# A seven-product matmul kernel: one of the four weight-block sums of each unit made by an accumulating DMA on Pool's queue

## The chip, the cores and the metric

One core of a Trainium2 chip runs the whole program. The metric is the device time of one execution in microseconds. Before the change the median of three runs is 978.04 us (976.92 to 979.71).

## The reference

The reference is a two-layer model of 256 tokens with 1024 features, all in float32. Each layer is a token mixer, a layer norm, a mixture of 16 experts and a second layer norm. Only the input projection of the first mixer matters here:

```python
def _mixer_ab(x, pos, w_in, ...):
    proj = x @ w_in          # [256, 1024] @ [1024, 6152]
    rq, rk, rv, rg, mq, mk, mv, mo, mi, mf = _split(proj, RET_SPLITS + ML_SPLITS)
    ...                      # retention on rq..rg, mLSTM on mq..mf
    return y @ w_out
```

## The kernel before, in words

The 6144 wide columns of this projection are cut into twelve units of 512 columns, ab0 to ab11. A unit's weights are 2 MB. SyncE (SP) loads them in two halves of 1 MB (rows 0 to 511, then 512 to 1023, L577 and L578) into one of six slots of `ring`, with the semaphores `ring_full` and `ring_rest`. A slot is loaded again when the unit in it has been used up (`freed`). The MoE weights follow through the same ring later on.

ab0 and ab1 (queries and keys of the retention, which VectorE then rotates by position, `rotate`) are multiplied in the plain way. ab2 to ab11 are the *seven-product units*: tokens (two blocks of 128) by inner dimension (two halves of 512) and inner dimension by columns (two blocks of 256) form 2x2 blocks, and seven block products take the place of eight, after Strassen and Winograd. A block product is 4 matmul calls of 128x256, or 8 of 128x128 in the two units whose result is kept with features on the partitions; the trace shows two instructions for each call. The blocks of a unit's weights are W11 (rows 0 to 511, columns 0 to 255), W12 (the same rows, columns 256 to 511), W21 and W22 (the rows below).

For each unit VectorE makes four sums of weight blocks, each one TENSOR_TENSOR of 128x1024. Three are in `mix_weights`: sums[1] = W22 - W12 (L2072), W12 := W12 - W11 in the slot itself (L2073), sums[0] = W22 - (the new W12) (L2076). The fourth is `mix_last` (L2083): W21 := W21 - sums[0], after the product of the old W21. Four sums of token blocks (`mix_tokens`, L2059, 128x512 each) are made once for all units: numbers 0 and 2 after the rotation of ab0, numbers 1 and 3 after that of ab1. `mix_weights` of ab2 stands between the two halves of the rotation of ab1.

TensorE's order in a unit (L813 for most units, L816 for the two of the other layout): the first product, W11 with the first token block (`first_product`, which is issued inside the unit before); then in `other_products` W21 with the first token block; sums[0] with token_mix[1]; sums[1] with token_mix[2]; W12 with token_mix[0]; the next unit's first product (`gap`); W22 with token_mix[3]; the corrected W21 with the second token block. Between products ScalarE copies the running sums out of the bank (`first_copy`, `sum_copy`, L1622) and VectorE adds the bank of another product to a copy (`blend`, L2095), in three steps for each unit. Semaphores carry this: `weights_mixed` (four for each unit), `tokens_mixed`, `product_done`, `first_copied`, `copied`, `combined`.

Every engine works through its program in order, and the order is written out by hand. On VectorE it is: rotate ab0, mix_tokens(0, 2), first half of rotate ab1, mix_weights(ab2), second half of rotate ab1, mix_tokens(1, 3), the gates of the mLSTM (from L2130), then for each unit blend 0, mix_last, blend 1, mix_weights of the next unit, blend 2, with the attention work of the finished heads between them. For ab6 and ab7 mix_weights of the next unit stands ahead of blend 1. ScalarE takes the Exp and Ln of the gates ahead of the first `sum_copy` of ab2.

GpSimd (POOL) has only DMAs on its queue in this stretch: parameter rows at L699 and L702, issued by 17.4 us, and then, after `y_done` has reached 8, the loads of the layer norm's rows (L725, L726), which are issued at 199.4 us.

Of the kernel before, what the change touches and what calls it, by code (L numbers as in the profile page):

```python
# [9 lines left out]
ALU = mybir.AluOpType  # L10
# [3 lines left out]
P = 128  # L14
SEQ = 256
# [87 lines left out]
def build(nc, a, out):  # L103
    with ExitStack() as ctx:
# [3 lines left out]
        def sem(name):  # L108
            return ctx.enter_context(nc.semaphore(name))
# [176 lines left out]
        tokens_mixed = sem("tokens_mixed")  # L286
        weights_mixed = sem("weights_mixed")
        first_done = sem("first_done")
        product_done = sem("product_done")
# [263 lines left out]
        def wait_unit(eng, name, t=None):  # L553

            eng.wait_ge(combined, 3 * fast[name] + (1 if t == 0 else 3))
            if t != 1:
                eng.wait_ge(copied, 3 * fast[name] + 3)

        block = ctx.enter_context(nc.Block())

# [136 lines left out]
        def _(pool):  # L697
# [3 lines left out]
            for dst, src in par_list[2:PAR_FIRST]:  # L701
                pool.dma_start(dst, src).then_inc(rows_in, 16)  # L702
            lns = [("ln_mix_g", "ln_mix_b", 0), ("ln_ffn_g", "ln_ffn_b", 0),
                   ("ln_mix_g", "ln_mix_b", 1), ("ln_ffn_g", "ln_ffn_b", 1)]
# [31 lines left out]
        def _(pe):  # L736
# [101 lines left out]
            def other_products(name, n, fill=None, gap=None):  # L838
# [8 lines left out]
                if fill:  # L847
                    fill()
                pe.wait_ge(weights_mixed, 4 * unit + 3)
                pe.wait_ge(tokens_mixed, 3)  # L850
# [4 lines left out]
                if unit:  # L855
                    pe.wait_ge(combined, 3 * unit)
                product(name, 2, token_mix[2], sums[1], True)
                pe.wait_ge(copied, 3 * unit + 1)
                product(name, 0, token_mix[0], weight_block(n, 0, 1), False).then_inc(product_done, 1)
                if gap:  # L860
# [3 lines left out]
                product(name, 0, token_mix[3], weight_block(n, 1, 1), False).then_inc(product_done, 1)  # L864
                pe.wait_ge(weights_mixed, 4 * unit + 4)
                pe.wait_ge(combined, 3 * unit + 2)
# [743 lines left out]
        def _(act):  # L1610
# [10 lines left out]
            def fn(o, i, f, **kw):  # L1621
                return nc.scalar.activation(o, i, f, **kw)  # L1622
# [18 lines left out]
            def first_copy(name):  # L1641

                act.wait_ge(first_done, fast[name] + 1)
                if name == "ab8":
                    act.wait_ge(weights_mixed, 4 * fast["ab7"] + 4)
                fn(place(name, 0, 0), held_part(name, 0), ACT.Copy).then_inc(first_copied, 1)

            def sum_copy(name, *which):

                for i in which:  # L1650
                    act.wait_ge(product_done, 5 * fast[name] + (2, 3, 4)[i])
                    fn(place(name, *((1, 0), (1, 1), (0, 1))[i]), held_part(name, 0), ACT.Copy).then_inc(copied, 1)

# [338 lines left out]
        def _(dve):  # L1992
# [58 lines left out]
            def mix_tokens(*which):  # L2051

                half = lambda t, kh: hT[:, 4 * kh:4 * kh + 4, t * P:(t + 1) * P]
                terms = ((half(1, 0), half(1, 1), ALU.add, 0), (token_mix[0], half(0, 0), ALU.subtract, 1),
                         (half(0, 0), half(1, 0), ALU.subtract, 0), (half(0, 1), token_mix[1], ALU.subtract, 3))
                for i in which:
                    x, y, op, done = terms[i]
                    dve.wait_ge(tokens_mixed, done) if done else None
                    V.tensor_tensor(token_mix[i], x, y, op).then_inc(tokens_mixed, 1)  # L2059

            def unit_weights(name):
                return ring[:, unit_no(0, int(name[2:])) % RING, :].rearrange("p (k n) -> p k n", k=KC)

            def mix_weights(name):

                unit, w, sums = fast[name], unit_weights(name), mixes(name)
                n = unit_no(0, int(name[2:]))
                dve.wait_ge(ring_full[n % RING], landed(n))
                dve.wait_ge(ring_rest[n % RING], landed(n))
                if unit:  # L2070
                    dve.wait_ge(product_done, 5 * unit - 2)
                V.tensor_tensor(sums[1], w[:, 4:8, SEQ:], w[:, 0:4, SEQ:], ALU.subtract).then_inc(weights_mixed, 1)  # L2072
                V.tensor_tensor(w[:, 0:4, SEQ:], w[:, 0:4, SEQ:], w[:, 0:4, 0:SEQ], ALU.subtract) \  # L2073
                    .then_inc(weights_mixed, 1)
                dve.wait_ge(weights_mixed, 4 * unit + 2)
                V.tensor_tensor(sums[0], w[:, 4:8, SEQ:], w[:, 0:4, SEQ:], ALU.subtract).then_inc(weights_mixed, 1)  # L2076

            def mix_last(name):

                unit, w, sums = fast[name], unit_weights(name), mixes(name)  # L2080
                dve.wait_ge(product_done, 5 * unit + 1)
                dve.wait_ge(weights_mixed, 4 * unit + 3)
                V.tensor_tensor(w[:, 4:8, 0:SEQ], w[:, 4:8, 0:SEQ], sums[0], ALU.subtract).then_inc(weights_mixed, 1)  # L2083

            def blend(name, *which):

                unit = fast[name]
                for i in which:
# [5 lines left out]
                    o = place(name, *((0, 0), (1, 1), (1, 0))[i])  # L2094
                    V.tensor_tensor(o, o, held_part(name, 1 if i == 0 else 2), ALU.add).then_inc(combined, 1)  # L2095

# [770 lines left out]
```

## Time and profile before

| what | value |
|---|---|
| median of three runs | 978.04 us (976.92 to 979.71) |
| the profiled execution, its time | 975.02 us |
| its span, first to last instruction | 973.1 us |
| TensorE matmuls busy | 940.3 us, 97% of the span |
| weight loads of TensorE | 549.6 us, 56% |
| VectorE | 358.4 us, 37% |
| ScalarE | 233.2 us, 24% |
| GpSimd | 15.2 us, 2% |
| granted TensorE clock, mean | 0.998 of full speed |
| DMA in the queues of SP, of Pool | 271.60 MB, 6.53 MB |

The profile is of one execution, and its own time, not the median of the runs, is what its rows add up to. TensorE's matmuls are pipelined, so a busy TensorE row says little about gaps; the idle time ahead of the weight loads (PEld) says more. An instruction's idle time is listed with what ended it, its releaser. A DMA has an issue time on the queue that starts it, and a time from issue to landing.

### The profile page before, as it was taken

To read this page: it belongs to the slowest core of one execution; us is meant where nothing else is said; L and a number is where in the kernel's file an instruction comes from. 1 tells how busy PE (TensorE), PEld (TensorE's weight loads), DVE (VectorE), ACT (ScalarE), POOL (GpSimd) and SP (SyncE) were. 2 spreads that over 40 slices of the span, in tenths; PEclk is the share of its full clock that TensorE was granted. 3 is DMA by queue.
4 is the path that set the end of the run, shared out by engine and by line. 5 is a ranking of instruction groups with operands and counts; after the bars stand their busy time and mean duration, and the time that the engine had idled before them with its cause. 6 is when DMAs were issued, how large, how long until landed. Compare 5 with 4: busy or idle time off the path is not lost.

```text
span 973.1 us, 10781 instructions
## 1 busy us (share of the span) xinstructions
PE 940.3 (97%) x4272; PEld 549.6 (56%) x4272; DVE 358.4 (37%) x847; ACT 233.2 (24%) x497; POOL 15.2 (2%) x29
## 2 busy tenths in 40 slices
PE   9999999999999999999999999999999999999996
PEld 8888988744533453333585568887545333443322
DVE  4666686523422121120335344644225220131204
ACT  1123353310311120110303353433513111111101
POOL 2000000000000000000000000000000000000001
PEclk9999999999999999999999999999999999999999
DMA  8984433453799999999995233444546899999994
GB/s 276 338 295 140 171 124 137 184 205 140 298 395 423 421 422 421 402 419 416 391 327 192 87 131 129 173 140 191 189 172 260 351 418 421 420 422 419 419 419 168
DMA packets 65782, 278.87 MB, mean 287 GB/s; under 512 B 8852, under 2 KB 9216, under 8 KB 41920
## 3 DMA queue, kind: packets, MB, share of 16 engines
q1 hardware_dynamic: 63856, 271.60, 71.1%
q0 software_dynamic: 1872, 6.53, 1.9%
q8 instruction: 37, 0.61, 0.2%
q14 instruction: 17, 0.14, 0.0%
HBM read 277.04 MB, written 1.06 MB: 286 GB/s over the span
## 4 chain that ended last, share of the span: by engine, by line
PE 79%; DMA 15%; DVE 3%; issue 1%; ACT 1%; SPq 0%; DVEq 0%
PE bank L746 63%; DMA ring<-in_moe_w_up 12%; PE bank L813 10%; DMA ring<-in_moe_w_down 2%; PE bank L1192 2%; PE bank L816 2%; DMA ring<-in_w_in_ab 1%; PE bank L1554 1%; PE bank L1197 1%; PE bank L905 1%; DVE feat L2280 1%; PE bank L1099 0%; ACT feat L1622 0%; PE bank L1140 0%; DVE stat L2589 0%
## 5 line engine op out<-in xcount | busy, mean ns | idle before, releaser
L746 PE MATMUL bank<-ring,feat 128*64 128x512 f32 (+1 forms) x1152 | 228.6, 595 | 3.0 <-ACT feat L1622 2.7
L746 PE MATMUL bank<-ring,hT 128*64 128x512 f32 (+1 forms) x544 | 161.0, 596 | 8.9 <-DMA ring<-in_moe_w_up 5.5
L746 PEld LDWEIGHTS bank<-ring,feat 128*64 128x64 f32 (+1 forms) x1152 | 74.2, 131 | 142.6 <-issue 131.0
L1622 ACT ACTIVATE feat<-bank 32x512 f32<-32x512 f32 (+3 forms) x128 | 60.8, 494 | 385.4 <-PE bank L746 241.3
L746 PE MATMUL bank<-hT,ring 128*128 128x256 f32 x640 | 140.1, 379 | 0.2 <-DMA ring<-in_w_in_ab 0.2
L746 PEld LDWEIGHTS bank<-hT,ring 128*128 128x128 f32 x640 | 121.8, 191 | 16.4 <-DMA ring<-in_w_in_ab 0.6
L746 PE MATMUL bank<-ring,yT 128*128 128x512 f32 x256 | 112.8, 595 | 0.0
L746 PEld LDWEIGHTS bank<-ring,hT 128*64 128x64 f32 (+1 forms) x544 | 59.3, 149 | 93.9 <-issue 87.1
L2579 DVE COPY feat<-bank 32x512 f32<-32x512 f32 (+1 forms) x56 | 38.5, 687 | 145.9 <-PE bank L746 145.4
L746 PEld LDWEIGHTS bank<-ring,yT 128*128 128x128 f32 x256 | 47.9, 190 | 55.3 <-issue 55.1
L2569 DVE TENSOR_TENSOR feat<-feat,bank 128x512 f32<-128x512 f32 x16 | 11.0, 688 | 172.7 <-PE bank L746 172.7
L1622 ACT ACTIVATE tok<-bank 128x256 f32<-128x256 f32 (+1 forms) x52 | 22.3, 431 | 133.7 <-PE bank L813 71.2
L813 PE MATMUL bank<-ring,hT 128*128 128x256 f32 x192 | 44.6, 380 | 0.0
L813 PEld LDWEIGHTS bank<-ring,hT 128*128 128x128 f32 x192 | 36.2, 190 | 5.6 <-issue 0.8
L746 PEld LDWEIGHTS bank<-tok,h 128*128 128x128 f32 x128 | 32.5, 331 | 11.4 <-issue 11.1
L746 PE MATMUL bank<-tok,h 128*128 128x256 f32 x128 | 37.6, 429 | 0.9 <-DVE tok L2456 0.9
L1622 ACT ACT_TABLE_LOAD x25 | 32.1, 1283 | 2.2 <-PE bank L746 1.7
L2291 DVE SCALAR_TENSOR_TENSOR feat<-bank,cols_cd,feat 128x255 f32<-128x255 f32 (+2 forms) x48 | 23.1, 481 | 25.7 <-ACT feat L1622 24.6
L1192 PE MATMUL bank<-feat 128*128 128x512 f32 x64 | 30.9, 607 | 1.0 <-ACT feat L1622 1.0
L813 PE MATMUL bank<-ring,yT 128*128 128x256 f32 x128 | 30.2, 379 | 0.0
L813 PEld LDWEIGHTS bank<-ring,yT 128*128 128x128 f32 x128 | 24.1, 190 | 3.1
L2095 DVE TENSOR_TENSOR tok<-tok,bank 128x256 f32<-128x256 f32 x30 | 12.5, 418 | 27.6 <-ACT tok L1622 21.5
(276 smaller groups left out, 802.5 us busy)
## 6 DMA issues: line engine op xcount, KB each, us to landing
ring<-in_moe_w_up SPq DMA_DIRECT2D x60, 1024.0 KB, 16.8
ring<-in_moe_w_gate SPq DMA_DIRECT2D x56, 1024.0 KB, 13.3
ring<-in_moe_w_down SPq DMA_DIRECT2D x56, 1024.0 KB, 12.1
ring<-in_w_in_ab SPq DMA_DIRECT2D x24, 1024.0 KB, 9.0
ring<-in_w_in_cd SPq DMA_DIRECT2D x24, 1024.0 KB, 13.6
ring<-in_w_out_ab SPq DMA_DIRECT2D x8, 1024.0 KB, 6.1
ring<-in_moe_w_down SPq DMA_DIRECT2D x16, 512.0 KB, 17.5
ring<-in_w_out_cd SPq DMA_DIRECT2D x8, 1024.0 KB, 6.0
```

The lines of the kernel that those rows point to most:

```text
L746: return nc.tensor.matmul(o, l, r, start=start, stop=stop)
L813: last = nc.tensor.matmul(o, x[:, k, :], y[:, k, :], start=first and k == 0, stop=k == 3, skip_group_check=True)
L816: last = nc.tensor.matmul(o[:, cols], y[:, k, cols], x[:, k, :], start=first and m == 0 and k == 0, stop=k == 3, skip_group_check=True)
L905: last = nc.tensor.transpose(bank[b][:, k * SEQ + t * P:k * SEQ + (t + 1) * P], src[:, t, c * P:(c + 1) * P], ident)
L1192: return nc.tensor.matmul(bank[4 + 2 * t + q][:, :], selw_t[:, t, :], ye[:, t, q * 512:(q + 1) * 512], start=start, stop=False, skip_group ...
L1197: last = nc.tensor.transpose(bank[0][:, c * P:(c + 1) * P], hid[:, c:FF:FF // P], ident)
L1554: last = nc.tensor.matmul(bank[b][e * SSD_HD:(e + 1) * SSD_HD, c * SEQ + j * P:(c + 1) * SEQ], xdt[:, j, hd * SSD_HD:(hd + 1) * SSD_HD], p ...
L1622: return nc.scalar.activation(o, i, f, **kw)
L2095: V.tensor_tensor(o, o, held_part(name, 1 if i == 0 else 2), ALU.add).then_inc(combined, 1)
L2291: ins = V.scalar_tensor_tensor(out=o, in0=bank[b][:, (m % 2) * SEQ:(m % 2 + 1) * SEQ - back], scalar=cols[:, c:c + 1], in1=o, op0=ALU.mult ...
L2569: V.tensor_tensor(hid, sil, bank[3][:, :], ALU.mult) \
L2579: ins = V.tensor_copy(ye[r, t, 512:1024], bank[3][r, :])
```

## The change

Pool's queue gets ten accumulating DMAs, one for each of ab2 to ab11, behind its parameter rows. When both halves of a unit's weights have landed, the DMA reads the W11 block (512 rows, 256 columns, 512 KB) once more from the input in device memory and adds it to the W12 block in the slot. Two semaphores `added`, used in turn, tell of it; from the third addition on Pool also waits for the one two before. `mix_weights` waits for `added` instead of the two ring semaphores and has two sums: sums[0] = W22 + W12', sums[1] = sums[0] - W11, where W12' is the block with W11 added. `mix_last` adds instead of subtracting. So that the signs come out right, the token sums become SCALAR_TENSOR_TENSOR with a factor of -1 (L2059), two of the three `sum_copy` of a unit copy with a scale of -1, and one `blend` of the three subtracts. `weights_mixed` now counts three for each unit. TensorE waits for the first sum ahead of the product with sums[0], for the second ahead of the product with sums[1], and for `added` ahead of the product with W12'.

```diff
@@ -285,6 +285,7 @@
         fix_ready = sem("fix_ready")
         tokens_mixed = sem("tokens_mixed")
         weights_mixed = sem("weights_mixed")
+        added = [sem(f"added{i}") for i in range(2)]
         first_done = sem("first_done")
         product_done = sem("product_done")
         first_copied = sem("first_copied")
@@ -556,6 +557,12 @@
             if t != 1:
                 eng.wait_ge(copied, 3 * fast[name] + 3)
 
+        def unit_weights(name):
+            return ring[:, unit_no(0, int(name[2:])) % RING, :].rearrange("p (k n) -> p k n", k=KC)
+
+        def wait_added(eng, name):
+            eng.wait_ge(added[fast[name] % 2], 16 * (fast[name] // 2 + 1))
+
         block = ctx.enter_context(nc.Block())
 
 
@@ -700,6 +707,20 @@
             pool.wait_ge(ring_rest[0], 16)
             for dst, src in par_list[2:PAR_FIRST]:
                 pool.dma_start(dst, src).then_inc(rows_in, 16)
+            def add_blocks(name):
+
+                unit, n = fast[name], unit_no(0, int(name[2:]))
+                pool.wait_ge(ring_full[n % RING], landed(n))
+                pool.wait_ge(ring_rest[n % RING], landed(n))
+                if unit > 1:
+                    pool.wait_ge(added[unit % 2], 16 * (unit // 2))
+                source, c0 = AB_UNITS[int(name[2:])]
+                pool.dma_start(unit_weights(name)[:, 0:4, SEQ:],
+                               a[source][0, 0:D // 2, c0:c0 + SEQ].rearrange("(k p) n -> p k n", p=P),
+                               accum_op=ALU.add).then_inc(added[unit % 2], 16)
+
+            for n in range(2, 12):
+                add_blocks(f"ab{n}")
             lns = [("ln_mix_g", "ln_mix_b", 0), ("ln_ffn_g", "ln_ffn_b", 0),
                    ("ln_mix_g", "ln_mix_b", 1), ("ln_ffn_g", "ln_ffn_b", 1)]
             for n, (g, b, l) in enumerate(lns):
@@ -846,7 +867,7 @@
                 product(name, 1, token_block(0, 1), weight_block(n, 1, 0), True).then_inc(product_done, 1)
                 if fill:
                     fill()
-                pe.wait_ge(weights_mixed, 4 * unit + 3)
+                pe.wait_ge(weights_mixed, 3 * unit + 1)
                 pe.wait_ge(tokens_mixed, 3)
                 pe.wait_ge(first_copied, unit + 1)
                 product(name, 0, token_mix[1], sums[0], False).then_inc(product_done, 1)
@@ -854,15 +875,17 @@
                     pe.wait_ge(stored[2], plan[name][2])
                 if unit:
                     pe.wait_ge(combined, 3 * unit)
+                pe.wait_ge(weights_mixed, 3 * unit + 2)
                 product(name, 2, token_mix[2], sums[1], True)
                 pe.wait_ge(copied, 3 * unit + 1)
+                wait_added(pe, name)
                 product(name, 0, token_mix[0], weight_block(n, 0, 1), False).then_inc(product_done, 1)
                 if gap:
                     gap()
                 pe.wait_ge(copied, 3 * unit + 2)
                 pe.wait_ge(tokens_mixed, 4)
                 product(name, 0, token_mix[3], weight_block(n, 1, 1), False).then_inc(product_done, 1)
-                pe.wait_ge(weights_mixed, 4 * unit + 4)
+                pe.wait_ge(weights_mixed, 3 * unit + 3)
                 pe.wait_ge(combined, 3 * unit + 2)
                 product(name, 2, token_block(1, 1), weight_block(n, 1, 0), False).then_inc(product_done, 1)
 
@@ -1642,14 +1665,15 @@
 
                 act.wait_ge(first_done, fast[name] + 1)
                 if name == "ab8":
-                    act.wait_ge(weights_mixed, 4 * fast["ab7"] + 4)
+                    act.wait_ge(weights_mixed, 3 * fast["ab7"] + 3)
                 fn(place(name, 0, 0), held_part(name, 0), ACT.Copy).then_inc(first_copied, 1)
 
             def sum_copy(name, *which):
 
                 for i in which:
                     act.wait_ge(product_done, 5 * fast[name] + (2, 3, 4)[i])
-                    fn(place(name, *((1, 0), (1, 1), (0, 1))[i]), held_part(name, 0), ACT.Copy).then_inc(copied, 1)
+                    fn(place(name, *((1, 0), (1, 1), (0, 1))[i]), held_part(name, 0), ACT.Copy,
+                       scale=-1.0 if i else 1.0).then_inc(copied, 1)
 
             def activate(name, f):
 
@@ -2051,36 +2075,31 @@
             def mix_tokens(*which):
 
                 half = lambda t, kh: hT[:, 4 * kh:4 * kh + 4, t * P:(t + 1) * P]
-                terms = ((half(1, 0), half(1, 1), ALU.add, 0), (token_mix[0], half(0, 0), ALU.subtract, 1),
-                         (half(0, 0), half(1, 0), ALU.subtract, 0), (half(0, 1), token_mix[1], ALU.subtract, 3))
+                terms = ((half(1, 0), half(1, 1), 0), (token_mix[0], half(0, 0), 1),
+                         (half(1, 0), half(0, 0), 0), (half(0, 1), token_mix[1], 3))
                 for i in which:
-                    x, y, op, done = terms[i]
+                    x, y, done = terms[i]
                     dve.wait_ge(tokens_mixed, done) if done else None
-                    V.tensor_tensor(token_mix[i], x, y, op).then_inc(tokens_mixed, 1)
-
-            def unit_weights(name):
-                return ring[:, unit_no(0, int(name[2:])) % RING, :].rearrange("p (k n) -> p k n", k=KC)
+                    V.scalar_tensor_tensor(out=token_mix[i], in0=x, scalar=-1.0, in1=y, op0=ALU.mult,
+                                           op1=ALU.add if i in (0, 2) else ALU.subtract).then_inc(tokens_mixed, 1)
 
             def mix_weights(name):
 
                 unit, w, sums = fast[name], unit_weights(name), mixes(name)
-                n = unit_no(0, int(name[2:]))
-                dve.wait_ge(ring_full[n % RING], landed(n))
-                dve.wait_ge(ring_rest[n % RING], landed(n))
+                wait_added(dve, name)
                 if unit:
                     dve.wait_ge(product_done, 5 * unit - 2)
-                V.tensor_tensor(sums[1], w[:, 4:8, SEQ:], w[:, 0:4, SEQ:], ALU.subtract).then_inc(weights_mixed, 1)
-                V.tensor_tensor(w[:, 0:4, SEQ:], w[:, 0:4, SEQ:], w[:, 0:4, 0:SEQ], ALU.subtract) \
-                    .then_inc(weights_mixed, 1)
-                dve.wait_ge(weights_mixed, 4 * unit + 2)
-                V.tensor_tensor(sums[0], w[:, 4:8, SEQ:], w[:, 0:4, SEQ:], ALU.subtract).then_inc(weights_mixed, 1)
+                    dve.wait_ge(weights_mixed, 3 * unit)
+                V.tensor_tensor(sums[0], w[:, 4:8, SEQ:], w[:, 0:4, SEQ:], ALU.add).then_inc(weights_mixed, 1)
+                dve.wait_ge(weights_mixed, 3 * unit + 1)
+                V.tensor_tensor(sums[1], sums[0], w[:, 0:4, 0:SEQ], ALU.subtract).then_inc(weights_mixed, 1)
 
             def mix_last(name):
 
                 unit, w, sums = fast[name], unit_weights(name), mixes(name)
                 dve.wait_ge(product_done, 5 * unit + 1)
-                dve.wait_ge(weights_mixed, 4 * unit + 3)
-                V.tensor_tensor(w[:, 4:8, 0:SEQ], w[:, 4:8, 0:SEQ], sums[0], ALU.subtract).then_inc(weights_mixed, 1)
+                dve.wait_ge(weights_mixed, 3 * unit + 2)
+                V.tensor_tensor(w[:, 4:8, 0:SEQ], w[:, 4:8, 0:SEQ], sums[0], ALU.add).then_inc(weights_mixed, 1)
 
             def blend(name, *which):
 
@@ -2092,7 +2111,8 @@
                     else:
                         dve.wait_ge(copied, 3 * unit + (2 if i == 1 else 1))
                     o = place(name, *((0, 0), (1, 1), (1, 0))[i])
-                    V.tensor_tensor(o, o, held_part(name, 1 if i == 0 else 2), ALU.add).then_inc(combined, 1)
+                    V.tensor_tensor(o, o, held_part(name, 1 if i == 0 else 2), ALU.subtract if i == 1 else ALU.add) \
+                        .then_inc(combined, 1)
 
             def rotate(name, first, between=None):
                 for q, b in enumerate(plan[name]):
```

## Rows read from the trace of the kernel before

**Rows 1.** The page: busy time of each engine, and the chain's shares by engine.
```profile
PE 940.3 (97%) x4272; PEld 549.6 (56%) x4272; DVE 358.4 (37%) x847; ACT 233.2 (24%) x497; POOL 15.2 (2%) x29
...
PE 79%; DMA 15%; DVE 3%; issue 1%; ACT 1%; SPq 0%; DVEq 0%
```

**Rows 2.** Weight loads' waits, 24 to 186 us: total, times, longest (us).
```profile
PEld bank L816 <- DVE feat L2076: 0.9, 1, 0.9
```

**Rows 3.** Chain that ended last, 122 to 128 us: start, duration (us), what.
```profile
122.64 1.13 DVE ring L2083
...
123.83 1.23 DVE feat L2072
125.06 1.15 DVE ring L2073
...
126.26 1.11 issue
127.37 0.42 DVE tok L2095
...
127.93 2.02 PE bank L816 x16
```

**Rows 4.** Groups by line and form, VectorE and ScalarE, 24 to 186 us.
```profile
L2231 DVE SCALAR_TENSOR_TENSOR spare<-bank,yT 128x384 f32<-128x384 f32 x4 | 2.1, 552 | 0.3 <-PE bank L746 0.3
...
L1622 ACT ACTIVATE feat<-feat 128x384 f32<-128x384 f32 x4 | 1.9, 514 | 0.0
L1622 ACT ACTIVATE yT<-consts 128x384 f32<-128x384 f32 x4 | 1.9, 510 | 0.0
```

**Rows 5.** Timeline, 33 to 51 us: start, duration (us), engine, line, what.
```profile
33.58 1.22 DVE L2072 TENSOR_TENSOR tok<-ring 128x1024 f32<-128x1024 f32 x1
...
38.48 0.69 DVE L2107 TENSOR_TENSOR yT<-bank,yT 128x512 f32<-128x512 f32 x1 [1.29 <-PE bank L746]
...
41.32 0.69 DVE L2059 TENSOR_TENSOR yT<-hT,yT 128x512 f32<-128x512 f32 x1
...
42.44 0.47 DVE L2130 TENSOR_SCALAR spare<-bank,ml_bias 4x256 f32<-4x256 f32 x1 [0.42 <-PE bank L746]
...
43.87 3.43 PEld L813 LDWEIGHTS bank<-tok,yT 128*128 128x128 f32 x16
...
46.01 0.38 ACT L1622 ACTIVATE tok<-bank 128x256 f32<-128x256 f32 x1
...
47.33 1.70 PEld L813 LDWEIGHTS bank<-ring,yT 128*128 128x128 f32 x8
...
50.73 1.21 DVE L2072 TENSOR_TENSOR tok<-ring 128x1024 f32<-128x1024 f32 x1
```

**Rows 6.** Issue of ab2's second half; landing times of its two halves.
```profile
L578 SPq DMA_DIRECT2D ring<-in_w_in_ab x1: 920/920/920, 22.1 to 22.1; - x1
...
DMA to landing us min/median/max: 5.1/6.5/8.0
```

**Rows 7.** Pool's DMAs issued at 199.4, 199.9, 474.6, 840.5, 841.0: KB, us to landing.
```profile
tok<-in_ln_mix_g POOLq DMA_DIRECT2D x1, 512.0 KB, 4.0
tok<-in_ln_mix_b POOLq DMA_DIRECT2D x1, 512.0 KB, 5.4
tok<-in_ln_ffn_g POOLq DMA_DIRECT2D x1, 512.0 KB, 6.6
tok<-in_ln_ffn_g POOLq DMA_DIRECT2D x1, 512.0 KB, 8.0
tok<-in_ln_ffn_b POOLq DMA_DIRECT2D x1, 512.0 KB, 12.7
```

**Rows 8.** Busy time in one stretch; last three: PEclk, DMA share, GB/s.
```profile
29.00:37.00 8.00, 8.00 (x39) 7.27 (x38) 5.29 (x6) 0.00 (x0) 0.00 (x0) 1.00 1.05 387
```

**Rows 9.** Timeline, issue of ab3's second half; and its time to landing.
```profile
23.94 0.53 SPq L578 DMA_DIRECT2D ring<-in_w_in_ab  x1
...
DMA to landing us min/median/max: 11.6/11.6/11.6
```

## The prediction

> **What bounds the kernel now.** I read the page first. TensorE is busy 97% of the span, and the chain that ended last is 79% TensorE, 15% DMA and 3% VectorE [rows 1]. So work taken off VectorE is worth something only where TensorE waits for it. Then I asked for the waits in 24 to 186 us, the stretch in which the ten seven-product units ab2 to ab11 run. VectorE makes all weight sums there, yet the weight loads of TensorE waited for it once, for 0.9 us [rows 2]. The chain shows that place: the last correction of ab7 (L2083), two of the three sums of ab8 (L2072, L2073), then the combination of ab7 (L2095), and only then, at 127.93, TensorE's last product of ab7, which waits for that combination (`combined`) [rows 3]. Everywhere else in this stretch VectorE is ahead.
>
> **Part 1, a sum less on VectorE.** Ten instructions of 128x1024 go, one per unit, each 1.15 to 1.23 us in the chain [rows 3]: about 12 us of VectorE. Nine of them lie beside TensorE's products and are worth nothing. The one of ab8 is in the chain: without it the combination that started at 127.37 starts some 1.15 us earlier and is done before TensorE asks. The most that this can give is the wait itself, **0.9 us** [rows 2]. I take all of it: VectorE did not wait between these pieces, so its data were there, and to 186 us the weight loads wait for VectorE or ScalarE nowhere else. The ends are 0 and 0.9.
>
> **Part 2, signs.** Four token sums of 128x512 become SCALAR_TENSOR_TENSOR. TENSOR_TENSOR of that size takes 0.69 [rows 5]; the nearest row of the new kind is 0.552 us for 128x384 [rows 4], 0.74 if scaled to 512. That is 0.05 each: +0.1 for the two that stand ahead of the gate work, counted in part 3. The other two stand ahead of a wait for TensorE and are hidden by it. The twenty copies with scale -1: an Exp of 128x384 with a constant scale (tables of decay, `yT`) takes 510 ns and one without (`feat`) 514 [rows 4], so nothing. The added waits of TensorE are on things that VectorE has waited for before it made the sums TensorE already waits for: nothing.
>
> **Part 3, ten accumulating DMAs on Pool's queue, and a wait for each on VectorE.** This decides. The one that matters is ab2's, as its weights arrive while they are wanted.
>
> *When it starts.* The second half of ab2's weights is issued at 22.1 and lands 8.0 us later [rows 6], at 30.1. Pool is free then and issues the addition at 30.3.
>
> *What waits behind it.* `mix_weights` of ab2 ran at 33.58 [rows 5]. Now VectorE stands there until the addition lands (call that L). Queued behind on VectorE: two sums (2.5 us: twice 1.23 [rows 3]), then the second half of the rotation and two token sums, which ran from 38.48 to 42.01 [rows 5] (3.5 us, now 3.6), and some 0.1 between them. So the gate work, which starts at 42.44, can start at L + 6.2 at the earliest. Behind it on ScalarE: Exp and Ln of the gates, and in program order behind these the copy of ab2 at 46.01, done at 46.39. TensorE's next product waits for this copy and started at 47.33 [rows 5]. Slack 0.9. So there is no stall while L + 6.2 is at most 42.44 + 0.9, that is **L up to 37.1**, and from there TensorE loses one us for each us. The product of the first weight sum, at 43.87 [rows 5], would bind later: its token sum ends 0.7 before the other, near L + 5.4, so L up to 38.4.
>
> *How long the addition takes.* No row shows an accumulating DMA. Near rows are Pool's own loads of 512 KB [rows 7]: 4.0 us with an idle queue, 5.4 for the one queued behind it, 6.6 and 8.0 while SP's stream of expert weights fills the engines, and 12.7 for the second of two then. The queues are full here: 387 GB/s at a share of 1.05 between 29 and 37 [rows 8]. Low end: the addition is like a plain load, 6.6, L = 36.9, no stall. High end: it must also read its destination, 1 MB in all, in 512 pieces of 1 KB where the plain loads have 128 of 4 KB. The row for 1 MB into full queues ends 0.5 + 12.7 = 13.2 us after the first issue: L = 43.5, stall 6.4. I take between: 4.0 for an idle queue, 1.4 for another 512 KB (5.4 less 4.0), 2.6 to 4.0 for the full queues (6.6 and 8.0, less 4.0), so 8.0 to 9.4, middle 8.7. L = 39.0, **stall 1.9 us**. No gain can come of this, as nothing waited for such a DMA before.
>
> *The nine others.* They move the next 5 MB through the queues, which delays the loads behind them by 1.3 to 3 us each. Cover: ab3 is the nearest. Its second half was issued at 23.94 and landed 11.6 us later [rows 9], at 35.5; even with the high end of 13.2 its addition lands by 49, where VectorE wants it at 50.73 [rows 5]. The later units are loaded further ahead of their sums. If this cover went, each would cost what ab2 costs. Pool's next work, the load of ln_mix, is issued at 199.4, long after. SP's queue gets nothing new; its later loads wait for slots that TensorE frees, so they move with TensorE.
>
> The Trainium skill (DMA: Bandwidth & Descriptors, Anatomy of one DMA — SWDGE path) puts a DMA of this queue at about 2.0 us plus its bytes at 436 GB/s. By that, an estimate, 512 KB take 3.2 us, L would be 33.5 and the stall nothing. The trace of this kernel does not agree: 4.0 us when idle, 6.6 and 8.0 when full [rows 7].
>
> **Sum.** -0.9 from part 1, nothing more from part 2, +1.9 from part 3: +1.0 us. The profiled execution spans 973.1 us and took 975.02; it becomes 976.0. It lies 3.0 below the median of the runs, 978.04; I forecast the median, **979.0**. About 0.3% (2.9 us) is what a measurement of this kernel can tell from no change.
>
> **Rivals.**
> A. *The addition is as fast as a plain load* (L at most 37.1; within 6.8 us of its issue). For it: 6.6 [rows 7]. Against: 8.0 in the same rows, more and smaller pieces, twice the reading. Then only the 0.9 counts: 977.1. The rule of the Trainium skill given above would have it so. Chance 0.22.
> B. *The accumulating DMA is slow, and ab2 waits*: the wait on `added` takes the place of the sum it removes. It is slower than before by over 2.9 when the stall passes 3.8, so L over 40.9, more than 10.6 us after issue. For it: 12.7 in full queues, the 1 KB pieces and reading of the destination. Against: 8.0 for the same bytes. Priced at the high end: 978.04 - 0.9 + 6.4 = 983.5. Chance 0.24.
> C. *The removed sum buys nothing*: at 127 another wait (a copy of ScalarE, the product's own data) ends just as late. Against: the chain between 122 and 128 runs on VectorE alone [rows 3]. With the forecast's stall: 979.9. Chance 0.05.
> D. *A gain that I do not see*: VectorE, 12 us lighter, also frees TensorE where the profile shows no wait. To pass 0.3% it must give 2.9 us where the waits of the stretch on VectorE sum to 0.9. Priced at the threshold, 975.1. Chance 0.04.
> The forecast, with L between 37.1 and 40.9 (net -0.9 to +2.9): chance 0.45.
>
> **How the numbers follow.** Faster by over 0.3%: D, 0.04, and 0.02 for chance shifts in the DMA-bound part: 0.06. Slower: B, 0.24. The rest, 0.70, is within 0.3%. Range: below, A at 977.1 less 1.1, as the three runs lie within 1.1 below their median and 1.7 above, 976.0; above, into B up to an L of 42.4, stall 5.3, 982.4. Left out: D and the upper half of B.
>
> **What the changed profile would show.** An accumulating DMA of 512 KB on Pool's queue issued near 30.3 and landing near 39; `mix_weights` of ab2 idle before its first sum, released by that DMA; the ScalarE copy of ab2 later than 46.4 and TensorE idle before the product behind it, about 2 us; no wait at the last product of ab7; `mix_weights` two instructions, never waiting for a DMA from ab3 on. Wrong if TensorE has no new wait before 48 us (A), if the landing takes over 10.6 us (B), if later units wait too, or if the wait of ab7 is still there (C).

## The result, and the profile after

The changed kernel takes 980.9 us (median of 20 runs, 978.25 to 984.3); the kernel before took 976.39 us in 20 runs beside them. The ratio is 1.0044 (95% interval 1.0034 to 1.0055): slower by 0.44%, some 4.3 us (3.3 to 5.4). That is a little more than the 0.3% from which the prediction counts a difference. The profiled execution took 982.04 us with a span of 980.2, against 975.02 and 973.1 before, so it is 7.0 longer and lies 1.1 above its own median; the one before lay 1.4 below.

The page of the changed kernel answers to [rows 1]: busy time, chain by engine, and Pool's queue.

```profile
PE 943.8 (96%) x4272; PEld 551.8 (56%) x4272; DVE 347.5 (35%) x837; ACT 233.2 (24%) x497; POOL 28.2 (3%) x39
...
q0 software_dynamic: 7152, 11.77, 5.3%
...
PE 80%; DMA 15%; DVE 2%; issue 2%; ACT 1%; SPq 0%; DVEq 0%
```

VectorE lost 10.9 us of work (358.4 before) and none of it shows in the time. TensorE's own busy time grew by 3.5 us, although it does the same matmuls: that is a lower clock, below. Next the weight loads' waits between 24 and 195 us, which answer to [rows 2], and below them VectorE's longest wait between 24 and 60 us.

```profile
PEld bank L834 <- issue: 4.0, 4, 2.9
PEld bank L767 <- DVE tok L2369: 1.2, 1, 1.2
PEld bank L767 <- issue: 1.0, 3, 0.3
...
DVE tok L2093 <- DMA ring<-in_w_in_ab: 7.8, 1, 7.8
```

The wait of 0.9 us for ab7's combination is gone from the list. A wait of 2.9 is new. The table puts it down to "issue", since the semaphore comes last from a VectorE instruction that ends just then. The timeline from 30 to 56 us, which answers to [rows 5], shows it (columns: start, duration, engine, line, operation, and in brackets the idle time before it):

```profile
30.59 1.35 POOL L718 DMA_DIRECT2D ring<-in_w_in_ab  x1 [12.33 <-DMA ring<-in_w_in_ab]
...
41.60 1.23 DVE L2093 TENSOR_TENSOR tok<-ring 128x1024 f32<-128x1024 f32 x1 [7.76 <-DMA ring<-in_w_in_ab]
42.43 1.59 PEld L834 LDWEIGHTS bank<-ring,hT 128*128 128x128 f32 x8 [0.43 <-issue]
...
46.12 0.69 DVE L2083 SCALAR_TENSOR_TENSOR yT<-yT,hT 128x512 f32<-128x512 f32 x1
46.84 0.69 DVE L2083 SCALAR_TENSOR_TENSOR yT<-hT,yT 128x512 f32<-128x512 f32 x1
46.88 5.00 PEld L834 LDWEIGHTS bank<-tok,yT 128*128 128x128 f32 x16 [2.85 <-issue]
47.45 0.47 DVE L2150 TENSOR_SCALAR spare<-bank,ml_bias 4x256 f32<-4x256 f32 x1
50.84 0.36 ACT L1645 ACTIVATE tok<-bank 128x256 f32<-128x256 f32 x1
51.91 1.70 PEld L834 LDWEIGHTS bank<-ring,yT 128*128 128x128 f32 x8
```

The addition for ab2 is issued at 30.59 and lands at 41.6; VectorE stands there for 7.8 us. Its queue then arrives late: the first of the two token sums (L2083) ends at 46.8, and TensorE, whose loads stand idle since 44.0, starts the products with the two weight sums at 46.88 (43.87 before, [rows 5]). The gates start at 47.45, ScalarE's copy at 50.84, the next product, the one with W12', at 51.91. The last product ahead of the wait is ab2's own product with the old W21, whose eight loads start at 42.43. From there to the product with W12' it is 9.48 us; before, it was 47.33 - 42.26 = 5.07, where 42.26 is the start of the same eight loads. **So ab2 costs TensorE 4.4 us.** The chain of waits of the changed kernel passes the same place with nothing of VectorE in it, only the gap (start, duration, what):

```profile
42.51 1.92 PE bank L834 x8
44.43 2.48 issue
```

The products with the two weight sums take 5.00 us instead of 3.43 [rows 5]. The windows of 2 us show why (columns: length, then busy time of PE, PEld, DVE, ACT and POOL, PEclk, DMA share, GB/s):

```profile
44.00:46.00 2.00, 0.43 (x2) 0.03 (x1) 1.90 (x4) 0.00 (x0) 0.00 (x0) 1.00 1.15 278
46.00:48.00 2.00, 1.09 (x3) 0.96 (x4) 1.90 (x5) 0.00 (x0) 1.28 (x1) 0.80 1.08 366
48.00:50.00 2.00, 2.00 (x6) 1.57 (x5) 0.75 (x2) 1.19 (x2) 0.00 (x0) 0.50 1.06 403
...
66.00:68.00 2.00, 2.00 (x7) 1.62 (x6) 0.00 (x0) 0.88 (x3) 0.60 (x1) 0.58 1.05 386
```

Behind the idle time the granted clock falls to 0.50, that is 1.2 GHz in place of 2.4, from 47.2 to about 50.6. A second such stretch follows at 64.3, under another group of sixteen loads (5.01 us where the profile of before has 3.32), with no more idle time ahead of it than the 0.33 us that stand there before as well. The profile of before has neither stretch.

The balance of the profiled execution, by TensorE's lag behind the kernel before at the same instruction: 0.2 at the start, 4.6 at 58.5 (4.4 at ab2), 6.3 at 83 (1.7, the second stretch), still 6.3 at 122, 5.6 from 130 on (0.7 given back at ab8), 5.7 to 6.0 up to 922, and 7.1 at the end. The last 1.2 to 1.4 arise in the expert stage. They need no addition to arise: measured in the same way, e4 below, in which Pool adds nothing, falls back by the same 1.3 there (0.6 at 915, 2.0 at 940).

ab8's place after the change (VectorE, then the loads of TensorE, which answer to [rows 3]):

```profile
128.83 1.22 DVE L2102 TENSOR_TENSOR ring<-ring,tok 128x1024 f32<-128x1024 f32 x1
130.55 1.23 DVE L2093 TENSOR_TENSOR feat<-ring 128x1024 f32<-128x1024 f32 x1 [0.50 <-DVE ring L2102]
131.81 1.23 DVE L2095 TENSOR_TENSOR feat<-feat,ring 128x1024 f32<-128x1024 f32 x1
132.96 0.41 DVE L2114 TENSOR_TENSOR tok<-tok,bank 128x256 f32<-128x256 f32 x1
...
133.48 1.86 PEld L837 LDWEIGHTS bank<-hT,ring 128*128 128x128 f32 x16 [0.20 <-issue]
```

The load waits 0.20 instead of 0.88. One sum is gone, but VectorE now idles 0.50 us itself, in the new wait for its own last correction (`weights_mixed` at 3 * unit), which stands ahead of the first sum. The experiments show that this is not the price of the wait as such (see e1).

Last the additions themselves: time to landing of ab2's, of ab3's and of ab11's (issued at 111.92, when the queues are empty), and the DMA packets by queue in two windows, 35.4 to 41.5 us and 113.5 to 118 us (q0 is Pool's, q1 SP's; packets, MB, share of 16 engines):

```profile
ring<-in_w_in_ab POOLq DMA_DIRECT2D x1, 512.0 KB, 11.0
ring<-in_w_in_ab POOLq DMA_DIRECT2D x1, 512.0 KB, 11.2
ring<-in_w_in_ab POOLq DMA_DIRECT2D x1, 512.0 KB, 5.9
...
q1 hardware_dynamic: 586, 1.17, 57.1%
q0 software_dynamic: 560, 0.56, 56.4%
...
q0 software_dynamic: 528, 0.52, 81.5%
```

The ten took 11.0, 11.2, 8.7, 8.9, 10.8, 12.1, 7.9, 10.0, 6.0 and 5.9 us in the order of the units. 528 packets for 0.52 MB: each of the 512 pieces of 1 KB travels as a packet of its own. In the full stretch Pool's packets and SP's, of 2 KB, leave in equal numbers.

### The profile page after: what moved, and what is told of

The parts are those of the page before. It is cut to its first block, busy times and chain, and to the rows that moved or that the text cites. A ratio compares the mean times of both kernels' runs of the same rounds, so it can differ in the third digit from the quotient of the medians.

```text
span 980.2 us, 10801 instructions
## 1 busy us (share of the span) xinstructions
PE 943.8 (96%) x4272; PEld 551.8 (56%) x4272; DVE 347.5 (35%) x837; ACT 233.2 (24%) x497; POOL 28.2 (3%) x39
## 4 chain that ended last, share of the span: by engine, by line
PE 80%; DMA 15%; DVE 2%; issue 2%; ACT 1%; SPq 0%; DVEq 0%
PE bank L767 63%; DMA ring<-in_moe_w_up 14%; PE bank L834 10%; PE bank L837 3%; PE bank L1215 1%; DMA ring<-in_w_in_ab 1%; PE bank L1577 1%; PE bank L1220 1%; PE bank L928 1%; PE bank L1122 0%; ACT feat L1645 0%; PE bank L1163 0%; DVE stat L2609 0%; DVE h L2851 0%; PE bank L1461 0%
## 5 line engine op out<-in xcount | busy, mean ns | idle before, releaser
L767 PEld LDWEIGHTS bank<-ring,hT 128*64 128x64 f32 (+1 forms) x544 | 59.5, 149 | 95.7 <-issue 88.1
```

The costliest lines, as they stand in the source:

```text
L767: return nc.tensor.matmul(o, l, r, start=start, stop=stop)
```

## The experiments

Theory S: ab2's late addition makes the loss, through VectorE's order, and nothing else does. Its rivals: the ten DMAs crowd the other loads; the changed signs or semaphores cost something by themselves; the idle time matters mainly through the clock behind it. "Loss at ab2" below is measured as above: start of ab2's product with the old W21 to start of its product with W12', less 5.07. "Before" is the kernel before, run beside each.

### e1: ab2's sum on VectorE, nine additions on Pool

```diff
-            for n in range(2, 12):
+            for n in range(3, 12):
 ...
             def mix_weights(name):
 ...
+                if unit == 0:
+                    dve.wait_ge(ring_full[2], landed(2))
+                    dve.wait_ge(ring_rest[2], landed(2))
+                    link(V.tensor_tensor(w[:, 0:4, SEQ:], w[:, 0:4, SEQ:], w[:, 0:4, 0:SEQ], ALU.add))
```

> Edit: VectorE makes the W12 sum of ab2 itself, the nine other additions stay DMAs. Theory 1 (the loss is the wait for ab2's addition, 4.4 us in the profile, and the two stretches at half clock behind it, 1.6 and 1.7 us): TensorE has no wait and no half clock before 70 us, the 0.7 us won at ab8 stay, so 0.7 us under the kernel before, ratio 0.999, mean clock 0.998. Theory 2 (the traffic of the additions or the new waits and signs cost by themselves): nine tenths of the loss stay, ratio 1.004.

Measured: 976.56 us against 976.96, ratio 0.9994 (0.9983 to 1.0005). The timeline has the product with W12' back in its place:

```profile
44.06 3.43 PEld L836 LDWEIGHTS bank<-tok,yT 128*128 128x128 f32 x16
47.52 1.70 PEld L836 LDWEIGHTS bank<-ring,yT 128*128 128x128 f32 x8
```

Loss at ab2: 47.52 - 42.45 - 5.07 = 0. One addition of ten carries the whole loss; the nine others, 4.5 MB, cost nothing that shows.

At ab8 this profile differs from the changed kernel's, though the code there is the same (VectorE's last correction of ab7, the first sum of ab8, then TensorE's loads of ab7's last product):

```profile
122.75 1.22 DVE L2108 TENSOR_TENSOR ring<-ring,tok 128x1024 f32<-128x1024 f32 x1
124.10 1.23 DVE L2099 TENSOR_TENSOR feat<-ring 128x1024 f32<-128x1024 f32 x1
...
127.13 1.87 PEld L839 LDWEIGHTS bank<-hT,ring 128*128 128x128 f32 x16
```

The sum starts 0.13 us behind the correction and not 0.50, the load waits for nothing, and TensorE gains 0.96 us on the kernel before, not 0.7. So it is in e1, e2, e5, e7, e8, e10 and e11; the 0.50 and the 0.7 stand in both profiles of the changed kernel, in e3 and in e6. The wait is the same in all, and why it takes 0.50 in some is open.

### e4: all sums on VectorE, only the signs and the order of the sums changed

```diff
-            for n in range(2, 12):
-                add_blocks(f"ab{n}")
 ...
-                wait_added(dve, name)
+                n = unit_no(0, int(name[2:]))
+                dve.wait_ge(ring_full[n % RING], landed(n))
+                dve.wait_ge(ring_rest[n % RING], landed(n))
+                link(V.tensor_tensor(w[:, 0:4, SEQ:], w[:, 0:4, SEQ:], w[:, 0:4, 0:SEQ], ALU.add))
```

> Edit: all ten sums back on VectorE as in-place additions, no DMA on Pool; signs, token sums and scaled copies as in the changed kernel. Theory 1: the same as the kernel before, ratio 1.000, with the wait of 0.9 us at the last product of ab7 back. Theory 2, if it is the signs: 1.004; if it is the traffic, 1.000 here and 1.004 in the run with nine DMAs.

Measured: 977.16 us, ratio 1.0001 (0.9988 to 1.0014). With the third sum back on VectorE, the wait for ab7's combination is back in the list of waits:

```profile
PEld bank L835 <- DVE feat L2095: 0.8, 1, 0.8
```

So the signs, the scaled copies and the waits on `weights_mixed` cost nothing that shows, and the removed sum does free that place. The waits on `added` are not in this kernel; e1 and e5 have them, at no loss.

### e2: the addition waits for the first half of the weights only

W11 and W12 both lie in the first half, so the addition doesn't need the second.

```diff
                 pool.wait_ge(ring_full[n % RING], landed(n))
-                pool.wait_ge(ring_rest[n % RING], landed(n))
 ...
+                dve.wait_ge(ring_rest[unit_no(0, int(name[2:])) % RING], landed(unit_no(0, int(name[2:]))))
                 wait_added(dve, name)
```

> Edit: each addition waits for the first half of its unit only (both blocks that it touches lie in it), VectorE waits for the second half itself. Theory 1 (TensorE loses one us for each us that the addition of ab2 lands after 37.1): the addition is issued at about 27.1 and not 30.6, takes 11 us again, lands at 38; the loss at ab2 falls from 4.4 to some 0.9 us. Ratio to before 1.000. Rival (what costs is not when it lands): ratio 1.003 or more.

Measured: 977.3 us against 976.89, ratio 1.0008 (0.9999 to 1.0017). In the timeline the addition starts 3.1 us earlier, at 27.52, and VectorE 2.7 earlier; TensorE's remaining wait is for ScalarE's copy:

```profile
27.52 1.35 POOL L717 DMA_DIRECT2D ring<-in_w_in_ab  x1 [9.45 <-DMA ring<-in_w_in_ab]
...
38.94 1.23 DVE L2093 TENSOR_TENSOR tok<-ring 128x1024 f32<-128x1024 f32 x1 [5.19 <-DMA ring<-in_w_in_ab]
...
48.59 1.59 PEld L833 LDWEIGHTS bank<-ring,yT 128*128 128x128 f32 x8 [1.05 <-ACT tok L1644]
```

The loss is 1.17, where 0.9 was expected. This is the rule of the prediction with another L: from VectorE's start to the product, 48.59 - 38.94 = 9.65 us.

### e3: ab2's two sums behind the rotation and the token sums

```diff
-            rotate("ab1", 4, lambda: mix_weights("ab2"))
+            rotate("ab1", 4)
 ...
             mix_tokens(1, 3)
+            mix_weights("ab2")
```

> Edit: on VectorE the two sums of ab2 stand behind the rotation and the token sums, not before. Theory 1: the addition still lands near 41.5, but only the gate work is behind it: the sums run from 42.2 to 44.7, the gates start 2.2 us late instead of 5.0, the loss at ab2 is 1.2 us. Ratio 1.0005. Rival (the addition costs wherever VectorE waits for it): 1.004.

Measured: 977.71 us, ratio 1.0008 (0.9996 to 1.0021). The addition takes as long as ever (10.9) and nobody waits for it, as the sums start at 42.26. The loss of 48.45 - 42.58 - 5.07 = 0.80 comes from the sums alone, which now stand ahead of the gates. I had expected 1.2. The order of VectorE's queue, and not the DMA's duration alone, makes the loss.

### e5 and e11: the first sum behind the token sums, the second behind the first gate instructions

```diff
-            rotate("ab1", 4, lambda: mix_weights("ab2"))
+            rotate("ab1", 4)
 ...
             mix_tokens(1, 3)
+            mix_weights("ab2", second=False)
 ...                                            (three gate instructions, L2154 on)
+            mix_weights("ab2", first=False)
             dve.wait_ge(gate_b, 1)
```

> Edit: the first sum of ab2 stands behind the token sums, the second behind the first three gate instructions, where VectorE waits 2.2 us for ScalarE. All ten additions stay on Pool's queue. Theory 1: no wait for the addition (it lands at 41.5, wanted at 42.2), the loss at ab2 is 0 to 0.3 us, the 0.7 us of ab8 stay: 0.5 us under the kernel before, ratio 0.9995. If ten additions cost by their traffic: 1.003.

> No edit against the split order: once more, to narrow its interval. Theory 1: 0.9993 to 0.9995. If the first result (0.9994, 0.9982 to 1.0006) was luck: 1.000 or more.

Measured: 976.31 us, ratio 0.9994 (0.9982 to 1.0006); the same kernel again 976.79, 0.9999 (0.9984 to 1.0014). All ten additions are kept, and the loss at ab2 is 0 (47.81 - 42.74 - 5.07). Yet the clock falls once in this kernel too, though no idle time beyond the usual 0.33 stands ahead (timeline and window of e5):

```profile
58.92 5.01 PEld L834 LDWEIGHTS bank<-tok,yT 128*128 128x128 f32 x16 [0.33 <-issue]
...
60.00:62.00 2.00, 2.00 (x6) 1.55 (x6) 0.00 (x0) 0.00 (x0) 0.00 (x0) 0.50 1.14 282
```

### e7: e2 and e5 together

```diff
-                pool.wait_ge(ring_rest[n % RING], landed(n))
 ...
+                dve.wait_ge(ring_rest[unit_no(0, int(name[2:])) % RING], landed(unit_no(0, int(name[2:]))))
                 wait_added(dve, name)
 ...                                            (and the order of e5)
```

> Edit: the two before together, order split and additions after the first half. Theory 1: the addition of ab2 lands at 38, 4 us before it is wanted, so also a late one costs nothing; time as in the split order or 0.2 us less, ratio 0.9993.

Measured: 977.15 us, ratio 1.0005 (0.9992 to 1.0017); loss at ab2 0. The two cures add nothing to each other, as either one alone leaves little or nothing to cure. The value expected lies inside the interval, near its end.

### e6: TensorE kept busy while it waits

Six more matmuls into a spare bank stand between ab2's product with the old W21 and the products with the sums, so that the addition is as late as ever and TensorE is not idle. They add work that the output doesn't use.

```diff
-    other_products("ab2", unit_no(0, 2), None, lambda: first_product("ab3", unit_no(0, 3)))
+    other_products("ab2", unit_no(0, 2), lambda: keep_busy(7, 6), lambda: first_product("ab3", unit_no(0, 3)))
```

> Edit: six extra matmuls of zeros (2.6 us) on TensorE while it waits for the first sum of ab2. Theory 3 (the half clock comes of TensorE standing idle for 2.5 us): both stretches at half clock go, mean clock 0.998, the weight loads behind the wait take 3.43 us for sixteen and not 5.0; the wait for the addition stays, now up to the copy of ab2. Ratio to before 1.002, where the changed kernel has 1.0044. Rival (the clock falls for another reason, DMA load or chance): clock near 0.995, ratio 1.004 or more.

Measured: 980.56 us, ratio 1.0039 (1.0024 to 1.0054). A miss: I had expected most of the clock's part back, 1.002. The timeline says why.

```profile
41.57 1.22 DVE L2093 TENSOR_TENSOR tok<-ring 128x1024 f32<-128x1024 f32 x1 [7.71 <-DMA ring<-in_w_in_ab]
...
46.84 3.32 PEld L834 LDWEIGHTS bank<-tok,yT 128*128 128x128 f32 x16 [0.20 <-issue]
51.22 1.59 PEld L834 LDWEIGHTS bank<-ring,yT 128*128 128x128 f32 x8 [1.05 <-ACT tok L1645]
```

The sixteen loads run at full clock, 3.32 us, and then TensorE waits 1.05 us for ScalarE's copy, a wait that the slow stretch had filled. The product starts at 51.22, 9.65 us after VectorE, just as in e2. Loss: 51.22 - 42.46 - 5.07 = 3.7 instead of 4.4. The lateness of VectorE's queue, not the clock, is most of the loss.

### e8: the same pieces by a plain DMA

For ab2 Pool's DMA copies the W11 block, in the same 512 pieces of 1 KB, into a buffer that is free then, and VectorE makes the sum in the time in which it would idle, and waits for the copy afterwards. What differs from the changed kernel is that nothing is accumulated, and with it, as the result shows, the size of the packets.

```diff
+                if unit == 0:
+                    pool.dma_start(conv_raw[:, 0:8:2, :], block).then_inc(added[0], 16)
+                    return
 ...                                            (and VectorE's own sum for ab2, as in e1)
```

> Edit: for ab2 Pool's DMA is a plain copy of the same 512 pieces of 1 KB into a free buffer, VectorE makes the sum in its idle time and then waits for the DMA as before. The accumulating DMA took 11.0 us, 4.8 to the first packet and 6.1 for 32 packets of 0.101 us per engine, each followed by one of 0.088 of SP's queue. If accumulating is what costs, packets of some 0.05 us, 9.3 us to landing, TensorE's loss at ab2 down by 1.7 us. If the size of the pieces is what costs, 11 us again.

Measured: 975.66 us, ratio 0.9985 (0.9973 to 0.9998). The copy lands after 7.2 us (timeline, DMA view, its packets between 31 and 38.3 us, and the two queues' packets while the copy's are on their way, 35.07 to 37.4 us):

```profile
38.20 1.23 DVE L2100 TENSOR_TENSOR tok<-ring 128x1024 f32<-128x1024 f32 x1 [3.01 <-DMA tok<-in_w_in_ab]
...
tok<-in_w_in_ab POOLq DMA_DIRECT2D x1, 512.0 KB, 7.2
...
q0 software_dynamic: 144, 0.52, 19.9%
...
q0 software_dynamic: 137, 0.52, 62.2%
q1 hardware_dynamic: 164, 0.33, 42.4%
```

144 packets for the same 0.52 MB, where the accumulating DMA has 528: the plain one puts four pieces into a packet. Loss at ab2: 47.84 - 42.65 - 5.07 = 0.12, and again 47.84 - 38.20 = 9.64. Neither of the two times that were expected came, 9.3 or 11, and the loss fell by 4.3 us and not by 1.7: the pieces did not stay apart, so this run changes two things at once. No run has a plain DMA in packets of 1 KB, and how much of the 11.0 us is the adding itself and how much the number of packets is not shown.

### e10: Pool adds for ab8 alone

```diff
-            for n in range(2, 12):
-                add_blocks(f"ab{n}")
+            add_blocks("ab8")
```

(with VectorE's own sum for the nine others, as in e4)

> Edit: Pool adds for ab8 alone, where TensorE waited for VectorE; VectorE makes all other sums. Theory 1 (only this one of the ten additions buys anything): the wait at the last product of ab7 is gone, no addition can come late, 0.7 us under the kernel before, ratio 0.9993. Rival (the lighter VectorE helps elsewhere too): this one is slower than the kernels with nine or ten additions and no wait at ab2.

Measured: 976.21 us, ratio 0.9991 (0.998 to 1.0002). There is no wait at ab2 and none at ab7's last product, and TensorE gains 0.96 us there. That is 0.1%, which an interval of 0.1% to either side can't show. The kernels with nine or ten additions and no wait at ab2 (0.9994, 0.9994, 0.9999) are no faster than this one with a single addition, so nothing speaks for a gain elsewhere from the lighter VectorE.

### e9: the changed kernel once more

> No edit: the changed kernel once more, for a second profile of the place at ab2. If standing idle is what lowers the clock there, this profile too shows a stretch at half clock behind the idle 2.5 us, where the profiles without that idle time (six of six so far) show none at that place; a second stretch further on may or may not come. Ratio 1.004 again.

Measured: 981.46 us against 977.03, ratio 1.0045 (1.0027 to 1.0062). The timeline repeats what the first profile of it showed:

```profile
42.34 1.23 DVE L2093 TENSOR_TENSOR tok<-ring 128x1024 f32<-128x1024 f32 x1 [8.22 <-DMA ring<-in_w_in_ab]
47.61 5.01 PEld L834 LDWEIGHTS bank<-tok,yT 128*128 128x128 f32 x16 [3.31 <-issue]
52.64 1.70 PEld L834 LDWEIGHTS bank<-ring,yT 128*128 128x128 f32 x8
```

The loss is 4.9 here, as the addition was issued 0.8 later. Its clock falls behind the idle time as well, at 48.8, and not again in the sixties. None of the versions beats the kernel before by an amount that I would trust. e8's interval ends just below 1, but at ab2 its VectorE makes all the sums that the kernel before makes and waits besides, and at the other units it is the same as e1 and e5, which are at 0.9994.

## Why the prediction was wrong where it was

The time, 980.9, lies in the range given (976.0 to 982.4), but the likeliest case, within 0.3%, is not what happened. The change is slower by 0.44%: rival B, with a chance of 0.24.

**The step that failed is the size of one term in part 3: "I take between: 4.0 for an idle queue, 1.4 for another 512 KB (5.4 less 4.0), 2.6 to 4.0 for the full queues (6.6 and 8.0, less 4.0), so 8.0 to 9.4, middle 8.7."** It took 11.0 us, landed at 41.5 instead of 39.0, and 10.9 to 11.3 in every kernel that kept it. The sum had priced the second 512 KB by a row of plain DMAs, and the full queues by rows of plain DMAs too. The first was nearly right: with an empty queue the addition needs 5.9 (ab11), and the estimate had 5.4. The second was not: the full queues add 5.1 (11.0 less 5.9), where the estimate had 2.6 to 4.0. Under load the 512 packets take turns with SP's, one for one, and that takes some 6 us; a plain DMA has only 128 packets to queue. e8, with the same bytes and pieces at the same place, has its 128 packets through in 2.3 us and lands after 7.2. That the number of packets makes the difference fits both counts but is argued, as e8 doesn't add either. The high end of 13.2 was not reached.

**The start** (30.3) was right to 0.3. **The rule of slack** (no stall up to L = 37.1, then one for one) held in form: e2, e6 and e8 place the product 9.65 us behind VectorE's start, whatever else is done. The text had 10.15 (6.2 to the gates, and 3.95 from there to the copy's end), too much by 0.5, most of it in the step to the gates (5.85); the two token sums, for one, take 0.69 us as SCALAR_TENSOR_TENSOR too, not 0.74. With L = 41.5 the rule gives 4.4, and 4.4 was measured, but partly by luck: the lateness alone is worth 3.7 (e6). The rule's figure reaches 4.4 by the 0.5 it has too much and by taking TensorE's start 0.2 too early; the measured one reaches it by 0.7 of lower clock, which the prediction did not have. The second stretch at half clock, 1.7 us, it did not have either.

**Part 1**, 0.9 us at ab8: 0.7 in the changed kernel, 0.96 in seven of the other profiles. I said that VectorE's data were there; in the changed kernel 0.5 us of idle time stand ahead of the sums, in the seven 0.1, behind the same wait. The wait of TensorE is gone in the changed kernel and back in e4, so rival C is excluded. **Part 2**, nothing for the signs: e4 at 1.0001 (0.9988 to 1.0014), right as far as an interval of 0.13% tells. **The nine others**, nothing: right, VectorE waits for no other addition, and e1 with nine of them is at 0.9994. Rival A, an addition as fast as a plain load, fell with the 11.0, and so did the figure of the Trainium skill quoted in the prediction, 3.2 us. D, a hidden gain of lighter VectorE, is excluded by e1 and e10.

Set against the medians: 3.7 of lateness and 0.7 of clock at ab2, less 0.7 at ab8, give 3.7 us, and 4.3 (3.3 to 5.4) was measured, so the interval leaves no remainder that needs a cause. The second half-clock stretch of the profile, 1.7 us, is not part of every execution. A stretch lowers the mean clock of an execution by 0.0017. The mean over the runs is 0.9952 and 0.9960 in the changed kernel (20 and 6 runs), 0.9963 and 0.9966 in the kernel before (35 and 23 runs beside e1 and e9). That is about half a stretch more in each execution, an estimate, and not two, and the kernel before has stretches too, though its profile shows none. The changed kernel's runs are spread over 6 us, those of before over 4.7 (974.99 to 979.71, without the one of 5020.71).

**Open.** Why the clock falls near 60 us. It did so in four profiles (64.3 in the changed kernel; 59.1, 59.5 and 59.7 in e5, e7 and e11) with no idle time ahead beyond the usual 0.33, and there not in e1, e2, e3, e4, e6, e8, e9 and e10. Idle time at ab2 is thus no condition for it. Of the fall at ab2 itself it can be said that both profiles with 2.9 and 3.3 us of idle time there have it, and no other has. That is two of two, no proof: e8's clock falls at 910.3, in the expert stage, behind loads that waited 2.8 us, and e6's loads wait 2.8 us at the same place and its clock does not fall.

## What to carry to other kernels

Before a sum is moved to an accumulating DMA, find the unit whose data arrive last before they are used: the saving is counted where the engine binds (one place of ten here), the delay where the data do (one place of ten too, and some 5 times as dear). If other queues are full, price such a DMA by its packets too, not by its bytes alone. Where one wait can't be avoided, put behind it, on its own engine, only what doesn't feed the critical engine: in e5 the same ten additions, each as slow as before, cost nothing that shows.

## What the runs showed of the hardware

- Accumulating DMAs keep their pieces apart: 512 packets of 1 KB (0.101 us each on an engine), where the plain DMA of the same pieces (e8) has 128 of 4 KB (0.18 us each). The Trainium skill (DMA: Bandwidth & Descriptors, SWDGE vs HWDGE vs iDMA) names 4096 bytes as the preferred upper size of a packet. The plain DMA fills it, the accumulating one stays at a quarter of it.
- Two queues take turns packet by packet: 586 packets of 2 KB against 560 of 1 KB in 6.1 us, and in e8 164 of 2 KB against 137, most of 4 KB, in 2.3 us. The Trainium skill (DMA: Bandwidth & Descriptors, Queues, rings and completion order) has an engine go round its queues at packet granularity, and the trace agrees. The engines move less in all beside the accumulating DMA: 283 GB/s in those 6.1 us, where e8 has 367 in its 2.3 us and SP's queue alone had 387 before [rows 8].
- The accumulating DMA holds Pool for 1.27 to 1.35 us at its issue, a plain one for 0.53, and 0.79 in e8. Under load ab2's first packet left 4.8 us after issue (4.2 for the plain copy of e8), ab11's, with empty queues, after 2.0.
- TensorE's clock fell to 1.2 GHz for 3.4 us in one piece: at ab2 behind 2.9 or 3.3 us of idle time, in e8 behind 2.8 us at 910, and in four profiles behind none but the usual 0.33. A stretch costs 1.6 to 1.7 us where TensorE has work throughout.
